# Two column groups of 256 and 304 in place of 304 and 256, with packed weight copies for the second group

## The reference, cut to what matters

```python
xn = rmsnorm(h, norm_mix); p = xn @ w_in          # 8 projections of 128 columns for each of 8 heads
GDN heads:  conv + silu, l2norm, gated delta rule  # o, S = chunked, exact per token
FoX heads:  softmax attention with decaying logits # causal, over meta + prompt; samples over cached pages too
h = h + concat(gdn, fox) @ w_out                   # 2048 x 2048
h = h + peer(rmsnorm(h))
def peer(x):                                       # per token
    s = (x @ w_query).reshape(8 heads, 2, 128) . sub_keys    # 2048 x 2048, then 128 keys on each side
    idx, gate = best 16 of the 16 x 16 sums of the two sides' best 16, softmax
    hid = gelu(x . expert_u[idx])                  # 16384 experts, rows of 2048
    return sum over 8 heads x 16 of gate * hid * expert_v[idx]
```

## Time and profile before

| | |
|---|---|
| median of 3 runs | 4961.61 us (4955.26 to 4962.0) |
| profiled execution | 4960.07 us |
| its span, first to last instruction | 4958.2 us |
| busy: PE / DVE / ACT / POOL | 2435.6 / 3370.0 / 541.9 / 2376.5 us |
| moved by DMA | 1480.39 MB |
| mean granted TensorE clock | 0.732 of full speed |

### The profile page before, as it was taken

One profiled execution on the slowest core, in us unless ns is written; L12 is line 12 of the kernel. 1 busy time (PEld: TensorE's weight loads), 2 busy tenths in 40 slices (PEclk: granted clock), 3 DMA queues, 4 the chain that ended last, 5 costly groups with the idle time before them and its releaser, 6 DMA issues. The chain is left out here.

```text
span 4958.2 us, 35078 instructions
## 1 busy us (share of the span) xinstructions
PE 2435.6 (49%) x11665; PEld 1945.6 (39%) x11665; DVE 3370.0 (68%) x4430; ACT 541.9 (11%) x1360; POOL 2376.5 (48%) x1230
## 2 busy tenths in 40 slices
PE   5999999979783877777764535310000000000000
PEld 4777777766663766666653434210000000000000
DVE  1233333330287588988886558988779998889888
ACT  1222222220001122222220000000000000000000
POOL 1000000000002366666656534447778887878886
PEclk8999999989896999888885767655555555555555
DMA  5655555513334799999998888878999999999998
GB/s 153 187 167 167 163 167 163 159 58 122 108 93 181 290 404 403 403 406 396 397 349 333 340 303 302 318 271 367 380 359 417 421 416 407 406 394 422 401 397 356
DMA packets 486235, 1480.39 MB, mean 299 GB/s; under 512 B 41180, under 2 KB 324624, under 8 KB 326520
## 3 DMA queue, kind: packets, MB, share of 16 engines
q0 software_dynamic: 162208, 1158.46, 58.2%
q1 hardware_dynamic: 314632, 252.58, 16.7%
q10 hardware_dynamic: 9216, 67.11, 3.3%
HBM read 1384.56 MB, written 93.32 MB: 298 GB/s over the span
## 5 line engine op out<-in xcount | busy, mean ns | idle before, releaser
L1778 DVE CUSTOM_DVE_ANT_0 ex_ring<-ex_ring,ex_xi 128x2048 f32<-128x2048 f32 x544 | 1244.3, 2289 | 160.2 <-DMA ex_ring<-in_peer_u_dram,idx_all 69.2
L1791 DVE SCALAR_TENSOR_TENSOR ex_y<-ex_ring,ex_wt,ex_y 128x2048 f32<-128x2048 f32 x539 | 1266.5, 2350 | 108.9 <-DMA ex_ring<-in_peer_v_dram,idx_all 81.6
L1729 POOL DMA_INDIRECT ex_ring<-in_peer_u_dram,idx_all x384 | 801.1, 2086 | 329.9 <-issue 109.3
L1729 POOL DMA_INDIRECT ex_ring<-in_peer_v_dram,idx_all x384 | 829.5, 2160 | 234.6 <-DVE ex_hid L1778 128.2
L785 PE MATMUL heads_a_pj<-xnT_a,heads_a_w 128*128 128x304 f32 x2048 | 622.1, 441 | 19.3 <-DMA heads_a_w<-in_w_in_dram 19.3
L785 PE MATMUL heads_b_pj<-xnT_b,heads_b_w 128*128 128x256 f32 x2048 | 548.7, 413 | 17.9 <-DVE mixT_b L1456 9.5
L1729 POOL DMA_INDIRECT ex_ring<-in_peer_v_dram,ex_idx_s x160 | 328.8, 2055 | 281.8 <-DVE ex_hid L1778 239.7
L785 PEld LDWEIGHTS heads_b_pj<-xnT_b,heads_b_w 128*128 128x128 f32 x2048 | 408.4, 211 | 73.9 <-DVE mixT_b L1456 12.6
L785 PEld LDWEIGHTS heads_a_pj<-xnT_a,heads_a_w 128*128 128x128 f32 x2048 | 380.4, 199 | 133.5 <-issue 23.0
L1729 POOL DMA_INDIRECT ex_ring<-in_peer_u_dram,ex_idx_s x160 | 300.2, 1877 | 208.8 <-DVE ex_y L1791 149.1
L1581 POOL TENSOR_TENSOR heads_a_ub<-heads_a_uN,const 128x1024 f32<-128x1024 f32 x8 | 15.2, 1896 | 559.0 <-ACT heads_a_uN L1176 559.0
(11 more groups left out here) (552 smaller groups left out, 3537.7 us busy)
## 6 DMA issues: line engine op xcount, KB each, us to landing
heads_a_w<-in_w_in_dram SPq DMA_DIRECT2D x64, 1024.0 KB, 6.0
w_scratch<-heads_a_w ACTq DMA_DIRECT2D x64, 1024.0 KB, 4.2
heads_b_w<-w_scratch SPq DMA_DIRECT2D x64, 1024.0 KB, 9.1
out_a_w<-in_w_out_dram SPq DMA_DIRECT2D x8, 2048.0 KB, 9.0
route_a_w<-in_peer_w_query_dram SPq DMA_DIRECT2D x16, 1024.0 KB, 5.9
out_b_w<-in_w_out_dram SPq DMA_DIRECT2D x8, 2048.0 KB, 29.8
route_b_w<-in_peer_w_query_dram SPq DMA_DIRECT2D x16, 1024.0 KB, 8.6
heads_a_kc<-in_cache_k_dram SPq DMA_DIRECT2D x128, 64.0 KB, 2.9
```

The lines of the kernel that those rows point to most:

```text
L1729: pool.indirect_dma_start(self.ring[:, i % RING, :], None, self.tables[which], bass.IndirectOffsetOnAxis(ap=self.index(s, g, k), axis=0)). ...
L1778: nc.vector.tensor_tensor_reduce(ring, ring, self.xi[:], 1.0, 0.0, ALU.mult, ALU.add, self.hid[:, g % 2, k:k + 1]).then_inc(self.sem["cons ...
L1791: nc.vector.scalar_tensor_tensor(y, ring, wt, y, ALU.mult, ALU.add).then_inc(self.sem["consumed"], 1)
```

## The change

FIRST becomes 256 columns in two tiles of 128, LATER 304 in tiles of 128, 128 and 48. The first 80 prompt tokens now share a tile with samples and meta tokens. The constants are split into a lasting part and one that only the first group holds. In the second group's heads stage there are 3 weight slots in place of 4.

In the first group, ScalarE writes each piece of w_out and of the query weights to contiguous scratch, and SP reloads a slot only when its copy is out; the second group loads both from scratch. The route has four weight slots in place of two.

The sets become: tile 1 of FIRST (8 groups); 64 prompt rows of FIRST's tile 0, in two halves by heads (4); samples (2); tile 0 of LATER (8); the other 16 prompt rows of FIRST's tile 0 with LATER's tile 2, in two halves by heads (4); tile 1 of LATER (8). That is 34 groups again. The order of items now restarts after the 14 groups of FIRST: these 448 items are all that can be gathered before `rest_of_experts`, and their last two groups end with v items alone. The quotas are 14, 330, 48, 8 and 48, which is 448, and 640 items are left. The index tables of the sets of LATER are spread by SP in `rest_of_experts`.

```diff
-FIRST = Group("a", 0, (0, 112, 240, 304), 0)
-LATER = Group("b", 304, (0, 128, 256), 3)
+FIRST = Group("a", 0, (0, 128, 256), 0)
+LATER = Group("b", 256, (0, 128, 256, 304), 2)
...
+            "w_out": nc.dram_tensor("w_out_scratch", (8, P, KT, 256), F32, kind="Internal").ap(),
+            "w_q": nc.dram_tensor("w_q_scratch", (2 * HEADS, P, KT, P), F32, kind="Internal").ap(),
...
-OVERLAP = {"norm": 12, "heads": 320, "out": 48, "ffn": 8, "route": 96}
+OVERLAP = {"norm": 14, "heads": 330, "out": 48, "ffn": 8, "route": 48}
...
-    W, PJ = (5, 3) if samples else (4, 2)
+    W, PJ = (5, 3) if samples else (3, 2)
...
-            (FIRST, [prompt_part(0, FIRST, 0), prompt_part(half, FIRST, 2)], HEADS),
+            (FIRST, [split(r, FIRST, 0, slice(T0, T0 + half)) for r in range(2)], HEADS // 2),
             (FIRST, [self.Part(r * NS, FIRST, 0, slice(0, NS), r * HEADS // fold, y_sample) for r in range(fold)], HEADS // fold),
             (LATER, [prompt_part(0, LATER, 0)], HEADS),
+            (LATER, [split(r, *p) for r in range(2) for p in ((FIRST, 0, slice(T0 + half, P)), (LATER, 2, slice(0, LATER.rows[2])))],
+             HEADS // 2),
             (LATER, [prompt_part(0, LATER, 1)], HEADS),
...
+        self.cut = max(s.end for s in self.sets if s.group is FIRST)
+        self.known = 2 * TOPK * self.cut
...
+    def run(self, g):
+
+        return (0, self.cut) if g < self.cut else (self.cut, self.groups - self.cut)
...
-        for i in range(self.issued, min(taken + RING, self.items)):
+        for i in range(self.issued, min(taken + RING, self.known)):
...
-            if r > 0 and part.slot == s.parts[r - 1].slot:
+            if any(part.slot == other.slot for other in s.parts[:r]):
                 pool.wait_ge(self.sem["y_out"], 16 * self.y_outs)
...
             for c in range(STEPS):
                 if c >= 2:
                     sp.wait_ge(sem["group_done"], (c - 1) * group.n)
-                sp.dma_start(w[:, c % 2], w_out[:, :, c * GW:(c + 1) * GW]).then_inc(sem[f"w_in{c % 2}"], 16)
+                    if group.samples:
+                        sp.wait_ge(sem[f"w_packed{c % 2}"], 16 * (c // 2))
+                sp.dma_start(w[:, c % 2], w_out[:, :, c * GW:(c + 1) * GW] if group.samples else scr["w_out"][c]
+                             ).then_inc(sem[f"w_in{c % 2}"], 16)
...
+            for c in range(STEPS if group.samples else 0):
+                act.wait_ge(sem[f"w_in{c % 2}"], 16 * (c // 2 + 1))
+                act.dma_start(scr["w_out"][c], w[:, c % 2]).then_inc(sem[f"w_packed{c % 2}"], 16)
...
+            for j in range(2 * HEADS):
+                if j >= 4:
+                    sp.wait_ge(sem[f"projected{j % 2}"], j // 2 - 1)
+                    if group.samples:
+                        sp.wait_ge(sem[f"w_packed{j % 4}"], 16 * (j // 4))
+                sp.dma_start(B.w[:, j % 4], w_q[:, :, j * P:(j + 1) * P] if group.samples else scr["w_q"][j]
+                             ).then_inc(sem[f"w_in{j % 4}"], 16)
...
                     nc.scalar.copy(B.q[:, s, :], pq[s][:, 0:N]).then_inc(sem[f"query_copied{s}"], 1)
+                    if group.samples:
+                        slot = (2 * h + s) % 4
+                        act.dma_start(scr["w_q"][2 * h + s], B.w[:, slot]).then_inc(sem[f"w_packed{slot}"], 16)
...
+        stream.known = stream.items
+
+        @block.sync
+        def _(sp):
+            stream.spread(sp, LATER)
```

More of the change, by code:

```diff
@@ L125, in constant_parts @@
         "row": row,
+        "valid": row < LATER.rows[-1],
+        "causal_mixed": np.where((row >= NS) & (first_keys > row - NS), NEG, 0.0),
+        "causal0": np.where(same0 & (col <= row) | (row >= NS), 0.0, NEG)[:, :NS],
+        "batch_cols": np.broadcast_to((np.arange(NS)[None, :] // NQ == np.arange(NB)[:, None]).reshape(1, -1),
+                                      (P, NB * NS)),
     }
@@ L596, in heads @@
     B = type("Buffers", (), buf)
-    pj, R1, R2, F = [buf[f"pj{i}"] for i in range(PJ)], B.R1, B.R2, (B.F2, B.F1)
+    pj, R1, R2, F = [buf[f"pj{i}"] for i in range(PJ)], B.R1, B.R2, (B.F2, B.F1) if samples else (B.F1, B.F2)
     w_in = ins["w_in"][0].rearrange("(k p) c -> p k c", p=P)
@@ L601, in heads @@
     gap = P - group.rows[0]
+    whole = N // P
     SEGMENTS = 8 * HEADS
@@ L759, in fox @@
                             sp.wait_ge(sem[f"f_{own}_copied"], n)
-                            sp.dma_start(out[group.seq:KW, h, :].rearrange("(t p) d -> p t d", p=P), rows[:]
+                            end = group.seq + whole * P
+                            sp.dma_start(out[group.seq:end, h, :].rearrange("(t p) d -> p t d", p=P), rows[:, 0:whole, :]
                                          ).then_inc(sem[f"{own}_kept"], 16)
+                            sp.dma_start(out[end:KW, h, :], rows[0:KW - end, whole, :]).then_inc(sem[f"{own}_kept"], 16)
             Marks(gdn(), fox(), weights(), *([cached()] if samples else [])).run()
@@ L1640, in __init__, with split @@
         half = P // 2
+        def split(r, group, tile, rows):
+            first = group.base + group.tiles[tile][0] - T0
+            p = r * half + (P - T0 - half if group is LATER else 0)
+            return self.Part(p, group, tile, rows, r * HEADS // 2, y_prompt[first + rows.start:first + rows.stop])
         fold = P // NS
@@ L1696, in gates, with spread @@
         return self.gate_s[:, at:at + TOPK]
-    def spread(self, sp):
+    def spread(self, sp, group):
         for s in self.sets:
-            for part in s.parts if not s.whole else []:
+            for part in s.parts if not s.whole and s.group is group else []:
                 for table, source in ((self.idx_s, self.mem["idx_all"]), (self.gate_s, self.mem["gate_all"])):
@@ L1705, in spread, with spread_all @@
                                  ).then_inc(self.sem["spread"], 16)
-    def spread_all(self):
-        return sum(32 * len(s.parts) for s in self.sets if not s.whole)
+    def spread_all(self, group):
+        return sum(32 * len(s.parts) for s in self.sets if not s.whole and (s.group is FIRST or s.group is group))
     def gather(self, pool, taken):
-        for i in range(self.issued, min(taken + RING, self.items)):
+        for i in range(self.issued, min(taken + RING, self.known)):
             which, g, k = self.item(i)
@@ L1769, in take @@
             which, g, k = self.item(i)
-            s, ring, turn = self.set_of[g], self.ring[:, i % RING, :], g + 2 * which
-            if i == self.turn_first(turn) and turn >= 2:
-                self.weigh(dve, turn - 2)
+            s, ring = self.set_of[g], self.ring[:, i % RING, :]
+            first, groups = self.run(g)
+            if which == 0 and k == 0 and g - first >= 2:
+                self.weigh(dve, g - 2)
+            elif which == 1 and k == 0 and g - first >= groups - 2:
+                self.weigh(dve, g)
             if which == 0:
@@ L1816, in gather, with mix_out @@
             self.stream.gather(pool, self.end)
-def mix_out(nc, ins, mem, group, stream, quota):
+def mix_out(nc, ins, mem, scr, group, stream, quota):
     mixT, hres = mem["mixT"], mem["hres"]
@@ L1969, in _, with route @@
                 last.then_inc(sem["keys_turned"], 1)
-def route(nc, ins, mem, group, stream, quota):
+def route(nc, ins, mem, scr, group, stream, quota):
     cst, xiT, skT = mem["cst"], mem["xiT"], mem["skT"]
```

104 lines of the change are left out of this document (56 added, 48 removed).

## The result

The changed kernel takes 4762.85 us (median of 4, 4751.76 to 4779.31) against 4959.82: ratio 0.9607, 95% interval [0.9574, 0.9639]. The forecast was 4790 us, with a range from 4690 to 4910, and its own range of 4740 to 4840 holds the time too. The profiled execution took 4779.31 us with a span of 4777.5 us, where 4786 was forecast.

The account below looks back on a forecast made before the run. TensorE was taken to bound the time before 1547 us, DMA the rest, with VectorE close behind. First group -307 and second group with last stage +135 made -172: span 4786, forecast 4790 us, range 4690 to 4910.

Parts of the forecast that it names:

- Head stage of the first group, -181: First group's heads: projections -112, level loops -39, other TensorE work -30 us; bounds -137 and -212.
- The projections' ratio of 0.82: First group's head projections: cost per record, 256 against 304 columns, 222.7 to 271.5 ns; 622.1 us become 510.
- Head stage of the second group, +88: Second group's heads: 1077 us grow to 1165, a third of the way from floor 1103 to 1295.
- The TensorE term: Second group's heads: projections 669 us plus about 334 of other work, 1003 us at clock 0.85.
- rival B: Second head stage keeps DMA's pace, 1103 us, and first group gives its upper bound: 4697 us; chance 0.16.
- Output stage of the second group, -27: Second group's output: contiguous w_out lands in 18 us, TensorE needs 180 plus 20 to start and end, 200 us.
- rival D: Second output stage: contiguous weights give nothing, 287 us; total 4877, up to 82 more if copies unhidden; chance 0.10.
- Last stage, +105: Last stage: 36 more items at 2.49 us make +90, waits between sets and restart +15.
- The +15 for waits between sets: Last stage: one more wait for sums and a stream restart, less some 11 us saved on samples' outs, net +15.
- C: Second head stage: TensorE keeps all its idle time, 1295 us; total 4920 us; chance 0.14.
- E: Second head stage: TensorE's waits come per tile, idle grows to 438, stage 1441 us, total 5066; chance 0.04.
- F: Whole kernel: second group gives back all 307 us the first saves, so the time stays; chance 0.03.

Follow-up runs that it names:

- second profile of the changed kernel: The changed kernel run again with nothing altered: 4756.08 us, ratio 0.9591 to the kernel before.
- the kernel that fills it: Against the changed kernel, the 330 items of the second head stage spread from its opening and projections on: 4730.29 us, ratio 0.954.

## Why the prediction was right, point by point

**What bounds each group.** Right: the first group follows TensorE, the second follows the stream. The two runs without items in the head stage and the one with 40 fewer show the second half for the head stage. That it is DMA's pace rather than VectorE's, as the prediction has it, stays open: each item takes both. The mirror of it, that what leaves TensorE in the first group leaves the span, is in the rows: its first head stage lost 152 us and TensorE's busy time there 156.

**Head stage of the first group, -181, measured -152.** Of the three parts, projections gave 88 us (622.1 to 534.2) where 112 were forecast, the level loops 21 (117.7 to 96.4) where 39, the rest 46 where 30; TensorE's idle time grew by 4. The projections' ratio of 0.82 was one mis-sized step: it was taken from two other stages, at granted clocks of 0.93 and 0.86. For the projections themselves, at equal clocks (0.94 before, 0.94 in the second profile of the changed kernel), it is 521.7 / 622.1 = 0.84, which is 256 / 304 and the prediction's own bound. That the two clocks made the difference is likely and not shown: corrected by them 0.82 becomes 0.89, past what was measured. The ratio is 12 of the 24 us that the projections fell short; the other 12 go with the clock of 0.90 in this execution. In the second profile the stage takes 850 us, -179. The level loops' third of 39 was mis-sized as well: with two tiles a record of L892 takes 35.9 / 192 = 187 ns of TensorE's time, with three it took 42.9 / 288 = 149. The runs without items show the same at nearly equal clocks of 0.98 and 0.99, in the second group: 30.7 / 192 = 160 ns with two tiles, 40.5 / 288 = 141 with three. So a record costs more where fewer independent tiles take turns, here by 13%.

**Output and route of the first group.** -52 and -60 forecast, -60 and -52 measured. The two misses cancel. The copies are hidden as costed; the runs with and without them show the same stages.

**Head stage of the second group, +88, measured +67.** The right end was chosen, by a reason that was only half right, so that 1165 came near 1144 is in part luck. The DMA term was good: 1048 us of transfer forecast, 0.93 x 1144 = 1064 measured. The TensorE term was not: 1003 us at clock 0.85 forecast, 930 at 0.90 measured (more on this in the last section). Its idle time was put at a third of the way between gone and kept. The runs show that there was no such part of its own: TensorE's idle time is what the stream leaves. What kept the stage from rival B's 1103 us was the thin start, and the kernel that fills it has 1115.

**Output stage of the second group, -27, measured -21.** The landing was put at 18 us and came to 11.9. That bought nothing more, since TensorE then sets the stage, with 170 us of work and 30 at the start where 20 were forecast for start and end. So rival D (contiguous weights give nothing) fell: with the groups kept as they are, reading contiguous weights gave 23, 28 and 40 us of this stage, though a transfer alone gives it no reason to (8.6 against 8.5 us). But D was priced too high: it kept the whole wait of 96.2 us and came to 287 us, while with the groups alone the stage took 229, with 51.1 us of waits. Even had the copies given nothing, the kernel would have been at 4787 us, where D has 4877.

**Last stage, +105, measured +87.** The 36 items cost VectorE 83 us where 90 were forecast at DMA's pace: 1490.5 us for 640 items against 1407.7 for 604. The +15 for waits between sets was mis-sized. VectorE's idle time in the stage is 214.5 us against 210.3, and the waits for sums are 32.6 us plus one of 16.9, which falls where GpSimd sends out the samples' sums before it goes on gathering; that is 49.5 together, against 26.1 + 23.1 = 49.2. The stage has three such waits in both kernels, not one more as the prediction has it: the wait that the extra set adds falls ahead of the stage. VectorE waited for sums once there before, 12.4 us, and twice now, 23.3.

**Rivals.** Of them B came nearest: 1144 us against its 1103. C (idle time kept whole, 1295) and E (1336 or more) did not happen: TensorE's wait for the masks fell from 87.3 us to 52.0 though there was a third tile. F, the pure exchange, is refuted by the first group's 282 us against 101.

## What to carry to other kernels

Decide for each stage which resource ends last, and move work out of the stages where it is alone into those where something else is the bound; then look whether the bounding resource is fed from the stage's first microsecond. Take ratios of costs from the line that they are for, at the same granted clock. Where a load shares the DMA engines with large gathers, larger pieces can pay (here 0.8% in the old groups), and where it runs alone they don't.

## What the runs showed of the hardware that was not expected

**The busy time of TensorE is not the same for the same work.** In the second head stage of the kernel before TensorE was busy 784.6 us at a granted clock of 0.85 with the stream beside it, and 676.8 us at 0.98 without. In the changed kernel it is 929.9 at 0.90 and 843.1 at 0.99. Busy time times clock agrees in both pairs (667 and 663, 837 and 835), and the forecast of 1003 us at 0.85 is 853 by this reckoning, 2% from 837. That is no rule. In the second output stage the old groups' 512 records took 120.1 us at 0.76 and 122.7 at 0.84 with the contiguous weights, products of 91 and 103: there the busy time is what stays, and the stage's clock is a mean over its idle time too. Nor is it the clock alone in the head stages: without the stream the projections fell only from 548.7 us to 497.1 and from 608.0 to 583.9, by 9 and 4%, and all other products from 235.9 to 179.7 and from 321.9 to 259.2, by 24 and 19%. How much of this is the clock, and how much that interrupted chains overlap less, stays open. For the forecast it means that a busy time read beside the stream overstates what TensorE needs alone.

**The clock of a steadily busy stage differs between executions** of one kernel, 0.92 in one and 0.95 to 0.98 in another over six heads' stretches, at the same busy share of 98%, and goes with the 27 us in the first head stage between two profiles of the changed kernel. What chooses between them stays open.

**The cost of small pieces is only in company.** 2 MB in pieces of 1 KB landed in 8.6 us alone, in 20.2 beside the gathers and in 29.8 in the kernel before; contiguous in 8.5 alone and 11.9 beside them. The gathers beside the contiguous load landed later, in 11.6 us against 9.5 (u items).
